# Expert stage of a hybrid trunk kernel: four units of 896 columns in place of seven steps of 512

## The reference

```
def moe_swiglu(x, w_router, we_gate, we_up, we_down):
    logits = (x @ w_router).astype(jnp.float32)
    top_vals, top_idx = lax.top_k(logits, TOP_K)          # 2 of 8 experts
    gates = jax.nn.softmax(top_vals, axis=-1)
    combine = jnp.einsum("bske,bsk->bse", jax.nn.one_hot(top_idx, N_EXPERTS), gates)
    out = jnp.zeros_like(x)
    for e in range(N_EXPERTS):
        out = out + combine[..., e:e + 1] * swiglu(x, we_gate[e], we_up[e], we_down[e])
    return out
```

## Time and profile before

| | |
|---|---|
| median of 3 runs | 1312.25 us (1312.14 to 1313.11) |
| the profiled execution | 1312.72 us |
| its span in the trace | 1311.0 us |
| bytes read from HBM | 428.66 MB |
| busy share of PE, DVE, ACT | 96%, 85%, 71% |
| mean TensorE clock granted | 0.994 of full |

### The profile page before, as it was taken

One profiled execution on the slowest core, in us unless ns is written; L12 is line 12 of the kernel. 1 busy time (PEld: TensorE's weight loads), 2 busy tenths in 40 slices (PEclk: granted clock), 3 DMA queues, 4 the chain that ended last, 5 costly groups with the idle time before them and its releaser, 6 DMA issues.

```text
span 1311.0 us, 15757 instructions
## 1 busy us (share of the span) xinstructions
PE 1259.0 (96%) x6233; PEld 1044.9 (80%) x6233; DVE 1116.1 (85%) x873; ACT 929.6 (71%) x734; POOL 56.9 (4%) x57
## 2 busy tenths in 40 slices
PE   9999999999999999999998999999999999999996
PEld 8988888889888888777776877787777777777875
DVE  6987555577889999899898989988989999889987
ACT  5575444464877887788777877877878887777763
POOL 1100000010002000000000000000000000000210
PEclk9999999999999999999999999999999999999998
DMA  9948555545669999999999999999999999999992
GB/s 325 339 140 277 188 188 187 191 153 198 209 209 360 394 394 386 396 394 393 394 394 397 394 396 385 394 394 394 395 397 394 394 394 394 396 392 393 397 394 87
DMA packets 204483, 435.52 MB, mean 332 GB/s; under 512 B 8196, under 2 KB 50228, under 8 KB 204404
## 3 DMA queue, kind: packets, MB, share of 16 engines
q1 hardware_dynamic: 200608, 421.06, 87.2%
q0 software_dynamic: 3712, 13.37, 3.0%
q10 hardware_dynamic: 84, 0.02, 0.0%
HBM read 428.66 MB, written 5.77 MB: 331 GB/s over the span
## 4 chain that ended last, share of the span: by engine, by line
DMA 40%; PE 38%; DVE 13%; ACT 7%; issue 2%; SPq 0%; DVEq 0%; ACTq 0%
DMA raw<-in_we_down 23%; DMA raw<-in_we_up 14%; DVE w_lo L972 11%; ACT w_hi L614 7%; PE turn L1730 4%; PE turn L1727 4%; PE accp L1618 4%; PE accp L1620 4%; PE accp L1619 4%; PE turn L1618 3%; PE turn L1620 2%; PE turn L1619 2%; DMA raw<-in_we_gate 2%; PE turn L1729 2%; PE turn L1728 2%
## 5 line engine op out<-in xcount | busy, mean ns | idle before, releaser
L972 DVE TENSOR_TENSOR w_lo<-raw,w_hi 128x2048 fp32r<-128x2048 f32 (+1 forms) x401 | 905.8, 2268 | 120.3 <-ACT w_hi L614 117.2
L614 ACT CAST w_hi<-raw 128x2048 fp32r<-128x2048 f32 x395 | 754.9, 1914 | 219.7 <-DMA raw<-in_we_up 75.7
L1618 PE MATMUL turn<-w_hi,a_hi 128*128 128x512 f32 x552 | 219.7, 398 | 4.1 <-DVE w_lo L972 4.1
L1620 PE MATMUL turn<-w_hi,a_lo 128*128 128x512 f32 x552 | 216.1, 391 | 0.0
L1619 PE MATMUL turn<-w_lo,a_hi 128*128 128x512 f32 x552 | 215.5, 390 | 0.0
L1981 PE MATMUL turn<-w_hi,t_both 128*128 128x512 f32 x336 | 135.5, 403 | 9.7 <-DVE w_lo L972 9.6
L1982 PE MATMUL turn<-w_lo,t_both 128*128 128x512 f32 x336 | 131.4, 391 | 0.0
L1618 PE MATMUL accp<-w_hi,hT_hi 128*128 128x512 f32 (+1 forms) x284 | 113.0, 398 | 19.1 <-DVE hT_lo L972 19.1
L1618 PEld LDWEIGHTS turn<-w_hi,a_hi 128*128 128x128 f32 x552 | 104.1, 189 | 27.3 <-DVE w_lo L972 6.3
L1620 PEld LDWEIGHTS turn<-w_hi,a_lo 128*128 128x128 f32 x552 | 103.9, 188 | 22.5
L1619 PEld LDWEIGHTS turn<-w_lo,a_hi 128*128 128x128 f32 x552 | 104.2, 189 | 20.6
(11 more groups left out here) (287 smaller groups left out, 1563.7 us busy)
## 6 DMA issues: line engine op xcount, KB each, us to landing
raw<-in_we_gate SPq DMA_DIRECT2D x112, 1024.0 KB, 11.5
raw<-in_we_up SPq DMA_DIRECT2D x112, 1024.0 KB, 11.7
raw<-in_we_down SPq DMA_DIRECT2D x112, 1024.0 KB, 11.5
raw<-in_w_in SPq DMA_DIRECT2D x18, 1024.0 KB, 8.4
raw<-in_w_down SPq DMA_DIRECT2D x11, 1024.0 KB, 5.1
raw<-in_w_gate SPq DMA_DIRECT2D x10, 1024.0 KB, 5.3
raw<-in_w_up SPq DMA_DIRECT2D x10, 1024.0 KB, 5.4
raw<-in_w_out SPq DMA_DIRECT2D x8, 1024.0 KB, 9.1
```

Of the source, the lines that this page charges most:

```text
L614: nc.scalar.copy(w_hi[:, p % PARTS, :], raw[:, p % RING, :]).then_inc(hi_done, 1)
L972: return nc.vector.tensor_tensor(out, whole, hi.bitcast(f32), ALU.subtract)
L1618: nc.tensor.matmul(to, lh, rh, start=start, stop=False, **group)
L1620: return nc.tensor.matmul(to, ll, rh, start=False, stop=stop, **group)
```

## The change

An expert goes in four *units* of 896 columns instead of seven steps of 512. 32 units take the place of 56 steps. Each unit has twelve pieces: gate in four, up in four (two k rows of 896 columns: 1792 columns a piece, 3.5 KB a row in HBM), and down in four (7 blocks of 128 rows: 2, 2, 2 and 1; the last piece is half as large). Rings keep their numbers of six and four buffers. Gate has two banks of 448 columns, up has two, and they don't alternate any more. h is turned into the gate's banks, in the middle of the next unit's up, after that unit's silu has left them. `h_e` has one buffer instead of two. Tokens of an expert are turned in one visit, in up's banks, after down. The first gate goes in three passes (all hi, all lo, then the low tokens) over four pieces. `ORDER` and the tables are rewritten for units.

The core of the diff (without the overflow branch and renamed buffers):

```diff
-    ORDER = "HHH" + "HLHLHHL" * 6 + "HLHLHLH" + "HHHH"
+    ORDER = "HHH" + "LHLHLHH" * 3 + "LLHLHHHH"
-    VISITS = ((3, 0, 0), (6, 1, 0), (7, 1, 1), (15, 2, 0), (18, 3, 0), (19, 3, 1), (25, 4, 0), (26, 4, 1),
-              (30, 5, 0), (38, 6, 0), (39, 6, 1))
+    VISITS = ((1, 0), (3, 1), (8, 2), (10, 3), (14, 4), (17, 5), (22, 6))
-    SUM_AT = (1, 5, 8, 12)
-    PICK_AT = 14
+    SUM_AT = (1, 2, 4, 6)
+    PICK_AT = 7
     def step_at(i):
-        return MOE_AT + (6 * i - 2 if i else 0)
+        return MOE_AT + (U_PIECES * i - 4 if i else 0)
-        def gate_bank(i):
-            return turn[:, 2 * (i % 2), :]
-        def up_bank(i):
-            return turn[:, 2 * (i % 2) + 1, :]
+        gate_banks, up_banks = (turn[:, 2 * i:2 * i + 2, 0:PART] for i in range(2))
+        hT_bank = turn[:, 0:2, :].rearrange("p b c -> p (b c)")[:, 0:WIDE]
+        tokens_bank = turn[:, 2:4, :].rearrange("p b c -> p (b c)")
```

SP's loads:

```diff
-                        for half in range(2):
-                            load(step_at(i) + 2 * j + half,
-                                 expert_rows(w, ORDER[i], k)[:, half * KD // 2:(half + 1) * KD // 2, s * COL:(s + 1) * COL])
+                        for pair in range(4):
+                            load(step_at(i) + 4 * j + pair,
+                                 expert_rows(w, ORDER[i], k)[:, 2 * pair:2 * pair + 2, s * WIDE:(s + 1) * WIDE])
```

ScalarE's queue for a unit (b is the unit's first piece; b+8 to b+11 are down of the unit before, b+12 on is the next gate):

```diff
-                if i:
-                    if light(i - 1):
-                        leave_up(i - 1)
-                    splits(b + 1, b + 2)
-                    if kept_at(i) is not None:
-                        keep_ys(kept_at(i))
-                    splits(b + 3, b + 4)
+                if kept_at(i) is not None:
+                    keep_ys(kept_at(i))
+                splits(b + 4, b + 6)
                 leave_gate(i)
...
+                splits(b + 7, b + 8)
+                if light(i - 1):
                     silu_few(i - 1)
-                    split_hi(b + 5)
+                    split_hi(b + 9)
                     round_few(i - 1)
-                    split_hi(b + 6)
                 else:
                     round_h(i - 1)
-                    splits(b + 5, b + 6)
-                after_up(i)
+                    split_hi(b + 9)
+                split_hi(b + 10)
+                if light(i):
+                    leave_up(i)
...
+                splits(b + 11, b + 14)
+                after_down(i)
+                if i < N_UNITS - 1:
+                    split_hi(b + 15)
```

TensorE:

```diff
-            for i in range(N_STEPS + 1):
+            for i in range(N_UNITS):
                 if i == 0:
                     first_gate()
-                elif i < N_STEPS:
-                    bank_read(i - 1)
-                    rows_step(i, 0)
-                if 0 < i < N_STEPS:
-                    turn_h(i - 1)
-                if i < N_STEPS:
+                else:
+                    for pair in range(4):
+                        rows_pair(i, 0, pair)
                     before_up(i)
-                    rows_step(i, 1)
+                for pair in range(4):
+                    if pair == 2 and i:
+                        amid_up(i)
+                    rows_pair(i, 1, pair)
                 if i:
-                    if i < N_STEPS:
-                        down(i - 1)
-                    else:
-                        last_down()
+                    down(i - 1)
+                after_down(i)
+            last_down()
+            def rows_pair(i, which, pair):
+                kind, (e, _) = ORDER[i], expert_step(i)
+                to = (gate_banks, up_banks)[which]
+                wh, wl = wide_rows(split(step_at(i) + 4 * which + pair))
+                for kk in range(2):
+                    k = 2 * pair + kk
+                    for c in range(2):
...
+                            last = product(to[:, c, :], (xg_hi[e % 2][:, k, :], xg_lo[e % 2][:, k, :]),
+                                           (wh[:, kk, c, :], wl[:, kk, c, :]), k == 0, k == KD - 1)
+                last.then_inc(piece_used, 1)
+            def before_up(i):
+                up_left(i - 1)
...
+            def amid_up(i):
+                gate_left(i)
+                if i in SUM_AT:
+                    sum_tokens(SUM_AT.index(i))
+                turn_h(i - 1)
+            def after_down(i):
+                if visit_at(i) is not None:
+                    up_left(i)
+                    turn_tokens(visit_at(i))
```

More of the change, by code:

```diff
@@ L1951, in fold_few @@
             def fold_few(i):
[L1953 to L1956 removed]
+                for to, a in ((gateT_bank, silu_e[:, i % 2, :]), (upT_bank, h_e[:])):
+                    for b in range(BLOCKS):
+                        last = nc.tensor.matmul(to[:, b * FEW:(b + 1) * FEW], a[:, b * P:(b + 1) * P], fold[:],
+                                                start=True, stop=True)
                 return last
@@ L1990, in few_half_down @@
                     for c in range(2):
                         cols = slice(c * BANK, (c + 1) * BANK)
-                        nc.tensor.matmul(accp[:, 2 + c, :], left, wh[:, j, cols], start=(first and j == 0), stop=False)
-                        last = nc.tensor.matmul(accp[:, 2 + c, :], left, wl[:, j, cols], start=False,
-                                                stop=(last_one and j == 1))
+                        nc.tensor.matmul(accp[:, 2 + c, :], hT_packed[:, block, :], wh[:, j, cols],
+                                         start=(first and block == 0), stop=False)
@@ new lines, in few_down_pair, with down_pair @@
+                        last = nc.tensor.matmul(accp[:, 2 + c, :], hT_packed[:, block, :], wl[:, j, cols], start=False,
+                                                stop=(last_one and block == BLOCKS - 1))
+                return last
+            def down_pair(pair, w, first, last_one):
+                wh, wl = [a[:, 0:len(blocks_of(pair)) * D].rearrange("p (j d) -> p j d", d=D) for a in w]
+                for j, block in enumerate(blocks_of(pair)):
+                    at = slice(block * P, (block + 1) * P)
+                    for c in range(2):
+                        cols = slice(c * BANK, (c + 1) * BANK)
+                        last = product(accp[:, c, :], [a[:, at] for a in (hT_hi, hT_lo)],
+                                       (wh[:, j, cols], wl[:, j, cols]), first and block == 0,
+                                       last_one and block == BLOCKS - 1)
@@ L2112, in first_gate @@
             def first_gate():
-                w = [[a.rearrange("p (k f) -> p k f", k=KD // 2) for a in split(MOE_AT + half)] for half in range(2)]
+                w = [wide_rows([a[:, (MOE_AT + pair) % PARTS, :] for a in (w_hi, w_lo)]) for pair in range(4)]
                 for k in range(KD):
@@ L2123, in first_gate @@
                         pe.wait_ge(xg_lo_ready, k // 4 + 1)
-                    last = nc.tensor.matmul(turn[:, 0, :], xg_lo[0][:, k, :], w[2 * k // KD][0][:, k % 4, :],
-                                            start=False, stop=(k == KD - 1))
-                    if k % 4 == 3:
+                    for c in range(2):
+                        last = nc.tensor.matmul(gate_banks[:, c, :], xg_lo[0][:, k, :], w[k // 2][0][:, k % 2, c, :],
+                                                start=False, stop=(k == KD - 1))
+                    if k % 2:
                         last.then_inc(piece_used, 1)
```

347 lines of the change are left out of this document (182 added, 165 removed).

## The result

The changed kernel takes 1321.91 us (median of four executions, 1319.11 to 1324.47) against 1312.59 before: ratio 1.007, interval 1.0052 to 1.0088. It is 0.7% slower, more than the noise; 1285 was forecast. The profiled execution took 1319.11 us for a span of 1317.3, predicted 1282.7. The 34.6 us between them lie in three places: down(30) ends at 1286.6 and not at 1256.7, of which 25 are there when unit 28 begins (it leaves its gate at 1174.7, some 10 us after its start, foreseen for 1139.4), the rest comes in units 28 to 30; and the end takes 30.7 us from there and not 26.0.

What follows compares the result with a forecast made beforehand. Transfer was taken as the bound, TensorE close behind. Transfer-bound middle units, TensorE-bound units 28 to 31 until 1256.7 and an end of 26.0 gave span 1282.7; with blocking and the median, 1285 us (own range 1277 to 1293, with rivals 1275 to 1305).

Steps and rivals of the forecast that it cites:

- Rival 1: Weight transfer: longer rows run no faster than 2 KB ones, or hardly; 27.9 us a unit, 1308 or 1300; chance 0.13.
- (c): Unit 0: the first gate takes all four split buffers at once, so up waits 1.15 us.
- (d): Unit 1: 0.8 us wait behind the expert ranking, then TensorE waits about 2 us before the first turn of tokens.
- (b): Twelve smaller pieces through ten ring buffers: slack of about 9 us, enough to ride over two heavy units in a row.
- sum of units 3 to 27: Middle of the expert stage: transfer sets the pace, 653.5 us for 24.25 units plus 16 for other traffic.
- (e): h turned within up: no wait while data is there; TensorE's 19.1 us wait for hT_lo should shrink.
- Rival 3: Each unit waits at the turn within up or at down; slower than before, 1318 to 1330; chance 0.08.
- Rival 2: Expert units: TensorE or VectorE becomes the bound through blocking, 1290 to 1309; chance 0.15.
- Rival 4: Expert ring: its change gains nothing because TensorE was the true bound; time within 0.2%; chance 0.03.
- (g): Units 29 and 30, adding kept rows: VectorE waits 3 us for the gathers, barely hidden by TensorE's split down pieces.
- (h): The end: TensorE waits 2.8 us and the longer last_down adds 4.2, so 26.0 us from the end of down(30).
- L: Follow-up theory: TensorE and VectorE take turns on a loop through the fold; the lighter heavy units gain 13 to 21 us.

Runs made afterwards that it cites:

- p1: Changed kernel with eight gate products entered twice in each heavy unit behind a light one (17.8 us more TensorE work): 1343.8 us.
- p3: Changed kernel with a spare VectorE subtraction of 1.67 us before piece b + 12's split in each heavy unit behind a light one: 1341.9 us.
- s5: Changed kernel with a seventh raw slot in the expert stage, all computation kept: 1319.8 us, ratio 1.0057 to the kernel before.
- b1: Kernel before, with eight gate products entered twice in eleven heavy steps behind a light one (20 us more TensorE work): 1313.2 us.
- s1: Changed kernel with VectorE taking 256 columns less of each gate and up piece from the second unit on: 1331.5 us.
- s2: Changed kernel loading one of two row groups in the last piece of gate and of up from the second unit on: 1317.5 us.
- s3: Changed kernel with ten products of each unit left out, two in gate and eight in up: 1319.6 us.
- s4: Changed kernel with twelve products left out of each heavy unit and twenty entered twice in each light one, TensorE's sum unchanged: 1311.1 us.
- e1: Changed kernel with the cast and split of piece b + 9 ahead of the light h's silu and product: 1327.8 us.
- e4: Changed kernel with h turned ahead of up again, silu and product ahead of piece b + 7: 1360.5 us.
- e2: Changed kernel with the high and low half of a heavy h ahead of the cast and split of piece b + 8: 1345.0 us.
- e3: Changed kernel with the first half of the last h rounded ahead of the last two pieces: 1321.9 us.

## Why the prediction was wrong

- **The prices held.** 448 columns come every 0.2025 us (predicted 0.200), the fold takes 3.08 (3.2), the full queue runs at 408 GB/s (27.0 us a unit; 26.95). Rival 1 is out.
- **(c), (d): the start held.** Up waits 1.54 us (1.15); at the first turn of tokens TensorE's weight load stands idle 1.1 us and its matmul 0.7 (2).
- **The step that failed is (b), "Slack is about 9 us", and with it the sum of units 3 to 27, with its "1 to 2 us for blocking".** It set a unit at the slowest of three (transfer 27.6 with other traffic, TensorE 26.8, VectorE 26) and took ten buffers for one slack that rides over all unevenness. The runs show a loop in its place, in which TensorE and VectorE take turns: 56.9 us for two units and not 55.2 (p1, p3). Six of the ten buffers are raw slots, ahead of ScalarE, and one more is worth nothing measurable (s5). Between VectorE and TensorE are only four pairs. Seven units take 199.4 us from 495.6 on and 200.0 from 695.0 on, 28.5 each; the 24 units from 495.6 to 1174.7 take 28.3 each, 0.7 over the 27.6: 17 of the 25 us that are missing at unit 28. The other 8 are there when unit 4 leaves its gate (495.6 and not about 487, by the same 27.6 a unit), and no run looks into them.
- **Why the loop is new is argued, not shown.** In steps of 512 columns TensorE's alternation was 16.8 and 12.7 us, 4 us and not 7, over as many buffers of nearly the same size, and the pairs of split buffers may have carried that and not this. b1 shows that the loop didn't bind there, and no run with more pairs and enough raw slots exists.
- **(e) held as it stands and looked the wrong way.** It asked only what TensorE waits for: TensorE does not wait for silu at the turn, and its wait for hT_lo shrinks (14.7 us for 19.1). What it left out is the reverse: ScalarE and VectorE stand until the fold is done (29.9 us, eleven times), with piece b + 9 and all that follows queued behind.
- **Rival 3 has the time by luck and the place half right.** It said 1318 to 1330 with a chance of 0.08. Its reason was TensorE waiting at the turn or at `down` in each unit, 55 us of idle time; TensorE waits 14.7 us at the heavy `down`, 6.3 at the light one and never at the turn. It compared 5.2 with 4.8 us of the light chain alone ("0.4 us is not 1.7") and did not follow the fold's release on to the next: ScalarE, twelve splits, low half, `down`. Rival 2 had the right kind of cause, blocking between near equals, and ended at 1309. Rival 4's reason, TensorE as the bound, is not shown: 63 us less of its work gave 2.
- **(g) failed in a term.** VectorE waits for the gathers less than it said, 0.92 and 1.16 us in unit 29, but it isn't hidden: TensorE then waits 1.1 and 0.3 us for split pieces, and it is 32.0 us between the exits from gate of units 29 and 30 (1204.45 to 1236.42), where 29.5 were foreseen.
- **(h) was too small by 4.7 us.** The last h stands behind one more piece, 382, than was counted: TensorE waits 4.75 us, not 2.8. And then the clock is at half, which costs another 2.0:

```profile
1291.55 0.79 PE L1644 MATMUL accp<-w_hi,hT_hi 128*128 128x512 f32 x1 [4.75 <-DVE hT_lo L997]
1292.14 0.63 PE L1645 MATMUL accp<-w_lo,hT_hi 128*128 128x512 f32 x1
1292.57 0.63 PE L1646 MATMUL accp<-w_hi,hT_lo 128*128 128x512 f32 x1
...
1295.55 0.62 PE L1644 MATMUL accp<-w_hi,hT_hi 128*128 128x512 f32 x1
1295.98 0.43 PE L1645 MATMUL accp<-w_lo,hT_hi 128*128 128x512 f32 x1
```

The matmuls start 0.427 us apart, and 0.227 before the wait. That is 4.0 of the 4.7; the rest is spread over the end. The longer `last_down` (4.2) is about as priced.

So the change did what it says to the transfer, about 1 us a unit where the queue is full. It was taken back by a loop through the fold that the kernel before did not run into, and the most likely reason is an alternation of light and heavy units coarser than four pairs of split buffers carry.

## What to carry to other kernels

Where several engines are within 10% of each other, don't take the largest sum for the period: follow one release (here the fold) through every in-order queue until it comes back, and add up that circle. A coarser step saves fixed costs but widens the swing between unlike steps. Compare the swing with the buffers between the two engines that swing, and not with all buffers of the pipeline; this case argues for that rule and doesn't prove it. To find the circle on the chip, put the same small work at two places and see where it passes in full. Relief says little where the next limit is 1 us away: none of s1, s2, s3 gave back what it took out. And look at where in the trace a gain falls before crediting a theory with it: s4's total came near to what L said, its rounds did not.

## What the runs showed of the hardware

- Waits of TensorE have a second price. After the 2.40 us wait above (a wait of 0.88 us had ended 1.5 us before it) the matmuls of s3 go from 0.23 to 0.43 us a piece from 879.2 to 882.6, some 1.6 us more. Taking 63 us of work from TensorE brought its mean granted clock from 0.995 to 0.977 in the profiled execution, with 88 matmuls at half clock, an estimate of 18 us, more than the 13 that the loop would have given. The two levels are those that the Trainium skill (TensorE: Matmul & The Clock Gate, Part 1: The HAM clock gate) names, 1.2 and 2.4 GHz. The rows agree: 0.427 us are 512 columns at 1.2 GHz, and 0.227 lie 14 ns above 512 columns at 2.4.
- Some of these kernels vary more from run to run than others. The kernel before lay within 2 us in every series, the changed one within 6, e1 within 14 and e4 within 17 (1349 to 1366), but e2, e3 and s2 within about 2 as well; what makes the difference is not shown.
